# Block inversion in a gated delta rule: four tiles in one step instead of two groups of two

## What is computed

```
a_mat = where(i > j, (k_beta @ k.T) * decay, 0)        # strictly lower, C x C
lhs   = a_mat + eye(C)
rhs   = concat([v * beta, k_beta * exp(g_cum)])
sol   = triangular_solve(lhs, rhs)                     # u, w
for each chunk n:
    v_new = u - w @ state
    o     = q_dec @ state + qk @ v_new
    state = state * exp(g_last) + k_dec.T @ v_new
```

## Time and profile before

| | us |
|---|---|
| median of 3 runs | 1878.14 |
| lowest, highest | 1876.71, 1883.59 |
| the profiled execution | 1875.73 |
| its span | 1874.0 |
| TensorE busy in the span | 1723.2 (92%) |
| VectorE busy | 1009.7 (54%) |
| ScalarE busy | 715.3 (38%) |
| GpSimd busy | 247.2 (13%) |
| granted TensorE clock, mean | 0.961 |

### The profile page before, as it was taken

One profiled execution on the slowest core, in us unless ns is written; L12 is line 12 of the kernel. 1 busy time (PEld: TensorE's weight loads), 2 busy tenths in 40 slices (PEclk: granted clock), 3 DMA queues, 4 the chain that ended last, 5 costly groups with the idle time before them and its releaser, 6 DMA issues.

```text
span 1874.0 us, 25796 instructions
## 1 busy us (share of the span) xinstructions
PE 1723.2 (92%) x9278; PEld 1345.2 (72%) x9278; DVE 1009.7 (54%) x1512; ACT 715.3 (38%) x1107; POOL 247.2 (13%) x216
## 2 busy tenths in 40 slices
PE   6899979999999969899768998999998899999999
PEld 4788757888888747457436776777776678888887
DVE  6456535444444562448666566665666444444443
ACT  6344423323232333214334444553554332323232
POOL 0244430000000120234110222111222000000000
PEclk8999979999999989999799999999998999999999
DMA  4222202333333323123002212221221123333333
GB/s 130 79 57 63 62 12 82 98 92 100 98 98 94 90 73 90 45 56 82 22 0 57 69 47 69 57 58 46 57 57 47 45 85 98 98 100 90 101 90 101
DMA packets 260239, 135.64 MB, mean 72 GB/s; under 512 B 12779, under 2 KB 257020, under 8 KB 260148
## 3 DMA queue, kind: packets, MB, share of 16 engines
q1 hardware_dynamic: 260148, 134.36, 25.7%
HBM read 132.16 MB, written 2.18 MB: 72 GB/s over the span
## 4 chain that ended last, share of the span: by engine, by line
PE 74%; issue 9%; DVE 7%; ACT 5%; POOL 3%; DVEq 0%; DMA 0%; ACTq 0%; POOLq 0%; PEldq 0%; SPq 0%; PEld 0%
PE bank L231 16%; PE bank L233 15%; PE bank L232 15%; PE bank L490 5%; PE bank L1603 4%; PE bank L492 4%; PE bank L491 4%; PE bank L1361 1%; PE bank L1172 1%; POOL arena L781 1%; PE bank L1113 1%; PE bank L1382 1%; POOL arena L798 1%; PE bank L1548 1%; ACT w_hi L211 1%
## 5 line engine op out<-in xcount | busy, mean ns | idle before, releaser
L215 DVE TENSOR_TENSOR w_lo<-raw,w_hi 128x1024 fp32r<-128x1024 f32 x219 | 278.7, 1273 | 110.6 <-ACT w_hi L211 107.6
L211 ACT CAST w_hi<-raw 128x1024 fp32r<-128x1024 f32 x235 | 246.1, 1047 | 231.5 <-PE bank L233 215.2
L231 PE MATMUL bank<-h_hi,w_hi 128*128 128x512 f32 x768 | 310.1, 404 | 25.2 <-DVE h_lo L993 10.4
L232 PE MATMUL bank<-h_lo,w_hi 128*128 128x512 f32 x768 | 303.0, 395 | 0.0
L233 PE MATMUL bank<-h_hi,w_lo 128*128 128x512 f32 x768 | 302.7, 394 | 0.0
L231 PE MATMUL bank<-m_hi,w_hi 128*128 128x512 f32 x608 | 239.4, 394 | 7.1 <-DVE w_lo L215 6.7
L232 PE MATMUL bank<-m_lo,w_hi 128*128 128x512 f32 x608 | 237.9, 391 | 0.0
L233 PE MATMUL bank<-m_hi,w_lo 128*128 128x512 f32 x608 | 237.7, 391 | 0.0
L490 PE MATMUL bank<-h_hi,w_hi 128*128 128x512 f32 x472 | 213.2, 452 | 6.5 <-issue 6.5
L231 PEld LDWEIGHTS bank<-h_hi,w_hi 128*128 128x128 f32 x768 | 146.7, 191 | 70.7 <-issue 19.1
L492 PE MATMUL bank<-h_hi,w_lo 128*128 128x512 f32 x472 | 187.2, 397 | 0.0
(11 more groups left out here) (272 smaller groups left out, 2261.0 us busy)
## 6 DMA issues: line engine op xcount, KB each, us to landing
raw<-in_l_w_ff SPq DMA_DIRECT2D x64, 512.0 KB, 4.0
raw<-in_w_in SPq DMA_DIRECT2D x64, 512.0 KB, 3.8
raw<-in_w_mlp_up SPq DMA_DIRECT2D x32, 512.0 KB, 3.9
raw<-in_w_mlp_down SPq DMA_DIRECT2D x32, 512.0 KB, 4.0
raw<-in_l_w_in SPq DMA_DIRECT2D x24, 512.0 KB, 3.8
raw<-in_l_w_out SPq DMA_DIRECT2D x8, 512.0 KB, 3.8
arena<-gb_rows SPq DMA_DIRECT2D x16, 256.0 KB, 3.9
raw<-in_w_out SPq DMA_DIRECT2D x8, 512.0 KB, 3.8
```

The source lines that it names most:

```text
L211: act.copy(w_hi[q.par][:], raw[q.par][:]).then_inc(s["w_hi_ready"], 1)
L215: dve.tensor_tensor(w_lo[q.par][:], raw[q.par][:], w_hi[q.par][:].bitcast(F32), ALU.subtract).then_inc(s["w_ready"], 1)
L231: pe.matmul(g_bank[q.par][:], w_hi[q.par][:, k], hi[:, k], start=(k == 0), stop=False)
L232: pe.matmul(g_bank[q.par][:], w_hi[q.par][:, k], lo[:, k], start=False, stop=False)
```

## The change

Each product of a level is made for all four tiles at once: Y into the bank `b[0]`, Z into `b[1]`. ScalarE copies one 128x256 block instead of two of 128x128, VectorE subtracts one 128x512 block instead of two of 128x256, and in level 0 each pair of 128x128 operations becomes one of 128x256. `t_all` holds the four T first and the four transposes behind them. The number of matmuls, their shapes and the work laid between them stay; their order within Y stays too, and within Z the first side of all four tiles comes before the second side. Waits and semaphore counts shrink with the groups: the next product waits for all four tiles.

The core of the diff (`@@` lines and untouched lines are left out in part):

```
-        NT = 4 + 2 * (LEVELS - 2) + 4
-        NZ = 2 * (LEVELS - 2) + 4
-        NY = 2 * (LEVELS - 1) + 1
+        NT = 2 + (LEVELS - 2) + 4
+        NZ = (LEVELS - 2) + 4
...
         def t_m(tt):
-            return t_all[:, 4 * (tt // 2) + tt % 2, :]
+            return t_all[:, tt, :]
...
         def t_t(tt):
-            return t_all[:, 4 * (tt // 2) + 2 + tt % 2, :]
+            return t_all[:, TT + tt, :]
...
-                    for f in range(2):
-                        bk = b[2 * f]
-                        if lv >= 1:
-                            pe.wait_ge(s["t_r"], NT * h + (3 if lv == 1 else 4 + 2 * (lv - 2) + 1) + f)
-                        pe.sem_inc(s["pe_go"], 1)
-                        for i in range(2):
-                            tt = 2 * f + i
-                            for c in range(2):
-                                r = part_of(c)
-                                rhs = half_masks[:, 0] if lv == 0 else t_m(tt)
-                                last = block(bk[r, i * CHUNK:(i + 1) * CHUNK], al[r, tt * CHUNK:(tt + 1) * CHUNK], rhs[r])
-                        last.then_inc(s["yy_ps"], 1)
+                    if lv >= 1:
+                        pe.wait_ge(s["t_r"], NT * h + 1 + lv)
+                    pe.sem_inc(s["pe_go"], 1)
+                    for tt in range(TT):
+                        i = slice(tt * CHUNK, (tt + 1) * CHUNK)
+                        rhs = half_masks[:, 0] if lv == 0 else t_m(tt)
+                        for c in range(2):
+                            r = part_of(c)
+                            last = block(b[0][r, i], al[r, i], rhs[r])
+                    last.then_inc(s["yy_ps"], 1)
...
                     eighth((6, 8, 9, 10, 12)[lv - 1])
+                    pe.wait_ge(s["y_sb2"], LEVELS * h + lv)
+                    pe.sem_inc(s["pe_go"], 1)
                     if lv < LEVELS - 1:
-                        for f in range(2):
-                            pe.wait_ge(s["y_sb2"], NY * h + 2 * (lv - 1) + f + 1)
-                            pe.sem_inc(s["pe_go"], 1)
-                            for side in range(2):
-                                for i in range(2):
-                                    tt = 2 * f + i
-                                    for c in range(2):
-                                        r = part_of(c)
-                                        o = b[2 * f + 1][r, (2 * side + i) * CHUNK:(2 * side + i + 1) * CHUNK]
-                                        left, right = (t_t(tt), y_m[:, tt]) if side == 0 else (y_m[:, tt], t_t(tt))
-                                        last = block(o, left[r], right[r])
-                            last.then_inc(s["z_ps"], 1)
+                        for side in range(2):
+                            for tt in range(TT):
+                                for c in range(2):
+                                    r = part_of(c)
+                                    o = b[1][r, (TT * side + tt) * CHUNK:(TT * side + tt + 1) * CHUNK]
+                                    left, right = (t_t(tt), y_m[:, tt]) if side == 0 else (y_m[:, tt], t_t(tt))
+                                    last = block(o, left[r], right[r])
+                        last.then_inc(s["z_ps"], 1)
...
                 def level(lv):
-                    for f in range(2):
-                        act.wait_ge(s["yy_ps"], (2 * LEVELS + 1) * h + 2 * lv + f + 1)
-                        act.copy(y_m[:, 2 * f:2 * f + 2], halves(b[2 * f][:, 0:2 * CHUNK], 2)).then_inc(s["y_sb2"], 1)
+                    act.wait_ge(s["yy_ps"], (LEVELS + 1) * h + lv + 1)
+                    act.copy(y_m, halves(b[0][:, 0:TT * CHUNK])).then_inc(s["y_sb2"], 1)
...
-                for f in range(2):
-                    dve.tensor_tensor(t_all[:, 4 * f + 2:4 * f + 4], eye, halves(a_lv[:, 0])[:, 2 * f:2 * f + 2],
-                                      ALU.subtract).then_inc(s["t_r"], 1)
-                for f in range(2):
-                    dve.wait_ge(s["yy_ps"], (2 * LEVELS + 1) * g + f + 1)
-                    dve.tensor_tensor(t_all[:, 4 * f:4 * f + 2], eye, halves(b[2 * f][:, 0:2 * CHUNK], 2),
-                                      ALU.subtract).then_inc(s["t_r"], 1)
+                dve.tensor_tensor(t_all[:, TT:2 * TT], eye, halves(a_lv[:, 0]), ALU.subtract).then_inc(s["t_r"], 1)
+                dve.wait_ge(s["yy_ps"], (LEVELS + 1) * g + 1)
+                dve.tensor_tensor(t_all[:, 0:TT], eye, halves(b[0][:, 0:TT * CHUNK]), ALU.subtract).then_inc(s["t_r"], 1)
...
                 for lv in range(1, LEVELS - 1):
-                    for f in range(2):
-                        dve.wait_ge(s["z_ps"], NZ * h + 2 * (lv - 1) + f + 1)
-                        dve.wait_ge(s["t_r"], NT * h + 4 + 2 * (lv - 1) + (f if lv > 1 else 0))
-                        dve.tensor_tensor(t_all[:, 4 * f:4 * f + 4], t_all[:, 4 * f:4 * f + 4],
-                                          halves(b[2 * f + 1][:, 0:TT * CHUNK]), ALU.subtract).then_inc(s["t_r"], 1)
+                    dve.wait_ge(s["z_ps"], NZ * h + lv)
+                    dve.wait_ge(s["t_r"], NT * h + 1 + lv)
+                    dve.tensor_tensor(t_all, t_all, halves(b[1][:], 2 * TT), ALU.subtract).then_inc(s["t_r"], 1)
```

More of the change, by code:

```diff
@@ L1484, in build @@
         o_sq, r_o, y_o = sq2[:, 0], rr[:, 0], sq2[:, 1]
-        NT = 4 + 2 * (LEVELS - 2) + 4
-        NZ = 2 * (LEVELS - 2) + 4
-        NY = 2 * (LEVELS - 1) + 1
+        NT = 2 + (LEVELS - 2) + 4
+        NZ = (LEVELS - 2) + 4
         def t_m(tt):
-            return t_all[:, 4 * (tt // 2) + tt % 2, :]
-        def t_m_all(r):
-            return t_all[r].rearrange("p (f s i) c -> p f s i c", f=2, s=2)[:, :, 0]
-        def t_t_all(r):
-            return t_all[r].rearrange("p (f s i) c -> p f s i c", f=2, s=2)[:, :, 1]
-        def pairs(ap):
-            return ap.rearrange("p (f i c) -> p f i c", f=2, c=CHUNK)
+            return t_all[:, tt, :]
         def t_t(tt):
-            return t_all[:, 4 * (tt // 2) + 2 + tt % 2, :]
+            return t_all[:, TT + tt, :]
         cleared += gla_sems + gate_sems
@@ L1669, in body @@
                 eighth(14)
-                pe.wait_ge(s["y_sb2"], NY * (h + 1))
+                pe.wait_ge(s["y_sb2"], LEVELS * (h + 1))
                 pe.sem_inc(s["pe_go"], 1)
@@ L1808, in body @@
                 level(5)
-                act.wait_ge(s["yy_ps"], (2 * LEVELS + 1) * (h + 1))
+                act.wait_ge(s["yy_ps"], (LEVELS + 1) * (h + 1))
                 bot = part_of(1)
@@ L2008, in body @@
                 top, bot = part_of(0), part_of(1)
-                nt = NT * h + 4 + 2 * (LEVELS - 2)
+                nt = NT * h + LEVELS
                 dve.wait_ge(s["t_r"], nt)
-                dve.wait_ge(s["z_ps"], NZ * h + 2 * (LEVELS - 2) + 1)
-                dve.tensor_tensor(t_f[bot, :, CHUNK:P].rearrange("p (f i) c -> p f i c", f=2), t_t_all(bot),
-                                  pairs(b[3][bot, 0:TT * CHUNK]), ALU.subtract).then_inc(s["t_r"], 1)
-                dve.wait_ge(s["z_ps"], NZ * h + 2 * (LEVELS - 2) + 2)
-                dve.tensor_tensor(t_m_all(top), t_m_all(top), pairs(b[1][top, 0:TT * CHUNK]), ALU.subtract).then_inc(s["t_r"], 1)
-                dve.wait_ge(s["z_ps"], NZ * h + 2 * (LEVELS - 2) + 3)
-                dve.tensor_tensor(t_f[top, :, 0:CHUNK].rearrange("p (f i) c -> p f i c", f=2), t_t_all(top),
-                                  pairs(b[2][top, 0:TT * CHUNK]), ALU.subtract).then_inc(s["t_r"], 1)
+                dve.wait_ge(s["z_ps"], NZ * h + LEVELS - 2 + 1)
+                dve.tensor_tensor(t_f[bot, :, CHUNK:P], t_all[bot, TT:2 * TT], halves(b[3][bot, 0:TT * CHUNK]), ALU.subtract).then_inc(s["t_r"], 1)
+                dve.wait_ge(s["z_ps"], NZ * h + LEVELS - 2 + 2)
+                dve.tensor_tensor(t_all[top, 0:TT], t_all[top, 0:TT], halves(b[1][top, 0:TT * CHUNK]), ALU.subtract).then_inc(s["t_r"], 1)
+                dve.wait_ge(s["z_ps"], NZ * h + LEVELS - 2 + 3)
+                dve.tensor_tensor(t_f[top, :, 0:CHUNK], t_all[top, TT:2 * TT], halves(b[2][top, 0:TT * CHUNK]), ALU.subtract).then_inc(s["t_r"], 1)
                 if front:
@@ L2098, in pool_gdn @@
                         if lv >= 2:
-                            pool.wait_ge(s["yy_ps"], (2 * LEVELS + 1) * h + 2 * lv - 2)
+                            pool.wait_ge(s["yy_ps"], (LEVELS + 1) * h + lv - 1)
                             if lv == 2:
-                                pool.wait_ge(s["t_r"], NT * h + 2)
+                                pool.wait_ge(s["t_r"], NT * h + 1)
                         pool.tensor_tensor(halves(a_lv[:, lv % 2]), a_tr, half_mask(lv + 1), ALU.mult).then_inc(s["al_r"], 1)
```

4 lines of the change are left out of this document (1 added, 3 removed).

## The result

| | before | after |
|---|---|---|
| median us | 1877.49 (8 runs) | 1895.51 (8 runs) |
| lowest, highest | 1872.32, 1883.59 | 1890.46, 1902.90 |
| profiled execution, its span | 1875.73, 1874.0 | 1901.44, 1899.6 |
| granted TensorE clock, mean of the span | 0.961 | 0.950 |

The ratio is 1.0092, with a 95% interval of 1.0071 to 1.0114: slower by 17 us (the two medians lie 18.0 apart). The forecast was slower by 9.9, 1888.0. The median lies half a microsecond above the range of 1881 to 1895, and the ratio times the median before, 1894.8, just inside it. Direction and mechanism held, the size did not. The profiled execution of the changed kernel is the second longest of its eight, 5.9 us above their median, so what its trace lost is more than the median lost.

The account below looks back on a forecast made before the run. TensorE's queue was taken to set the pace, with the time from Z's end to the next Y counting. Heads 0 to 6 lose 8.5 us and the last 1.4, 9.9 in all: 1878.1 + 9.9 = 1888.0 us, range 1881 to 1895.

Parts of the forecast that it names:

- TensorE's queue sets the pace: Inside a head: TensorE works 18.75 of 19.0 us; VectorE and ScalarE matter only by when they hand over.
- the rest of the head hangs on the same chain: Behind the levels of a looped head: nothing takes the shift of 1.25 us at full clock back.
- The price of the hand-over: In the levels: one 128x512 subtraction takes 0.69 us, so Z's end to the next Y is 0.97 us.
- Per looped head 1.2 to 1.25: Loss in a looped head's levels: 1.25 us at full clock, about 1.2 in head 0 or at low clock.
- ScalarE's share: Before Z(1) in a looped head: one merged copy instead of two shifts Z(1) by 0.1 us.
- The turn: First level, VectorE alternating with GpSimd: merging gains nothing between looped heads and 1.2 us before the last head.
- The bare levels of the last head: Levels 2 to 4 and Y(5), without eighths: 10.8 us against 8.24, a loss of about 2.6 us.
- a rival with plus 4.5 us: TensorE's clock: longer waits may bring three more low stretches, plus 4.5 us, 1892.5; chance 0.17.
- one of minus 4.5: TensorE's clock: waits at other moments may bring three fewer low stretches, 1883.5 us; chance 0.12.
- Busy time deciding: VectorE's queue sets the pace, each head saves 2.3 us, 18 us in all, 1860; chance 0.05.
- The turn going to VectorE in all heads: Between heads line 2074 gets in before GpSimd's mask; heads 1 to 6 gain up to 1.2 us each, 1880.8; chance 0.13.

Follow-up runs that it names:

- run 7: Kernel before, with every eighth from the seventh on laid one place earlier, eighth(7) in the wait before Z(1): ratio 1.0011.
- run 9: Changed kernel, with one more eighth between Z(3) and Y(4), later eighths one place earlier: ratio 1.0100 against the kernel before.
- run 4: Changed kernel, with unread added matmuls in the last head and 8 before Z(1) in every head: ratio 1.0046 against the kernel before.
- run 1: Kernel before, with only Y of all four tiles in one bank and one ScalarE copy per level: ratio 1.0038.
- run 3: Changed kernel, with unread added matmuls in the last head only: ratio 1.0063 against the kernel before.
- run 6: Kernel before, with unread added matmuls in the last head alone, none behind Z: ratio 0.9998.
- run 5: Changed kernel, with level 0 in halves again on VectorE: ratio 1.0094 against the kernel before.
- run 2: Kernel before, with only Z of all four tiles in one bank and one 128x512 subtraction per level in levels 1 to 4: ratio 1.0066.
- run 8: Kernel before, with level 0 alone merged and Y(0) four products of the panel earlier: ratio 0.9970, median 1873.57 us.

## Why the prediction was right, and where it was too small

**What bounds the kernel.** Half right. VectorE and ScalarE do wait for TensorE in the levels, and VectorE's busy time, which fell from 1009.7 to 995.9 us, was worth nothing. But "TensorE's queue sets the pace" does not hold for the whole head. Runs 7 and 9 took an eighth out of the last stretch of a head, and that stretch did not get shorter. Part of TensorE's busy time (92% of the span) is thus work laid into waits. The account that fits, argued and not shown, is that a head is a ring of hand-overs: inversion, recurrence, output, first products of the next head. The runs show two of its signs, that 1.25 us of latency put into the levels was paid in full and that moving an eighth gained nothing; they do not trace the ring link by link. The prediction came to the first sign by saying that the rest of the head hangs on the same chain and nothing takes the shift back. That was right, but it did not follow from a queue that sets the pace.

**The price of the hand-over.** Right. 0.69 was taken and 0.686 measured; 0.97 us from Z's end to the next Y, 0.97 measured before Y(4); 13.3 us from Z(1) to Y(5), 13.32 measured at full clock (run 4). The formula in the section on the TRN2 errata of the Trainium skill, "VectorE: DVE Perf Modes", gives an estimate of 0.69 us, and the 0.686 of the trace agrees; the advice there to make tiles large cost time here, since the engine that it relieves was waiting. Per looped head 1.2 to 1.25 was forecast; at full clock it is 1.25 (18.02 against 16.77), with a low stretch on both sides 1.2 (19.5 against 18.3). Heads 0 and 6 cost 0.9 each (18.3 against 17.4; 17.6 in run 4 against 16.7), less than the forecast's 1.2. Heads 0 to 6 come to 8.0 us of latency, where 8.5 was forecast. ScalarE's share was put at 0.1, and run 1 has 0.1.

**Between heads and the last head.** The turn was called right: no gain above 0.4 us in heads 0 to 5, 1.3 before the last (35.2 against 36.6), where 1.2 was taken. The bare levels of the last head were forecast at 2.6 us more; filled and at full clock (run 3) its whole length is 3.3 above that of before, 2.7 above the filled one of before (run 6).

**The clock.** This is the term that was mis-sized. It stood as a rival with plus 4.5 us and a chance of 0.17, offset by one of minus 4.5, so the forecast held nothing for it. In the trace of the changed kernel it is three more low stretches in the looped heads, 1.5 us each, 4.5 us, and about 10 us in the last head (46.4 against 36.5 filled). That execution lies 5.9 us above the median; by the estimate at equal mean clock the clock's share in the medians is 3 to 5 us, close to the rival's 4.5. The prediction treated the low stretches as a matter of where the 2.1 us wait falls, as likely to be fewer as to be more. All six looped heads from 1 to 6 had one in the changed kernel and in runs 3 and 5, five in run 9 and four in run 2, against three before, three in run 1 and two in run 6. The last head varies more: it was at the low clock for 10.2 us before, 37.5 us (from 1442 on) in the changed kernel, 23.9 us in runs 5 and 9, but 10.3 us in run 2, with the merged subtraction, and 20.4 us in run 8, without it. One trace of each does not show how much of this the change brings.

The parts at full clock add up to 8.0 us in the looped heads, less 1.3 for the turn, plus 2.7 in the last head: 9.4 us, and 9.9 was forecast. With 3 to 5 us of the clock that makes 12 to 14 of the measured 17; where the remaining 3 to 5 us lie is not shown.

**The rivals.** Busy time deciding is refuted by the result. The turn going to VectorE in all heads did not happen in the changed kernel; it takes Y(0) earlier, as run 8 shows. Whether the six low stretches of heads 1 to 6 come from the longer waits in the levels or from where the period of a head now puts the old wait is not settled: the wait before Z(1) is 2.1 us in both kernels, it stayed without a low stretch in three heads before, in four of run 6 and in one of run 9, and nothing here changed the period alone.

## What to carry to other kernels

Two groups that hand over to each other are worth their extra instructions as long as the chain is bound by hand-overs: the fixed cost of an instruction is paid by an engine that waits anyway, while the last element of a merged instruction comes later. Before merging, ask which of the two is short, time on the engine or time to the result. And where a stretch has no work to lay into its waits, price the clock of TensorE too: here it added 3 to 5 us in the median, by the estimate above, and some 14 in the profiled execution.

A busy share of 92% does not show that an engine sets the pace; take a piece of its work away and look whether the stretch gets shorter. Here moving one small product earlier, so that the engine behind it asked for its turn in time, gained 0.3% (0.9970, with level 0 merged as well), and laying more of the panels' work into the waits gained nothing.

## What the runs showed of the hardware

VectorE operations whose two inputs lie in SBUF and GpSimd operations take turns whole: a 128x512 one on VectorE (0.69 us alone) ended 0.54 to 0.56 us behind the end of GpSimd's instruction in six cases of six (two each between heads 2 and 3 before, before the last head after, and between heads 2 and 3 in run 8). GpSimd's 128x256 mask, 0.72 us long at 1207.69 us before, took 1.17 to 1.18 where it stood behind such an operation. An operation with one input in PSUM kept its length beside GpSimd: line 2001 at 1219.62 us before, 0.42 us while GpSimd worked. The Trainium skill, "SBUF — State Buffer", in its list of terms, calls the shared port pair locked and held for the full instruction; these rows agree with the taking of turns.

The granted clock of the last head was 0.98 in 1444 to 1482 us of run 3, with 34 added matmuls between 1437 and 1459 us, and 0.51 in 1442 to 1480 us of the changed kernel, which has the same instructions apart from them. The Trainium skill, "TensorE: Matmul & The Clock Gate", in "What's actually happening", says that the low clock is the default and activity lifts it; the two numbers agree. The waits alone do not tell what an execution gets. The same wait of 2.1 us before Z(1) was followed by the low clock in six heads of six in the changed kernel, in three of six before, and in two of six in run 6, whose looped heads are those of before.
